# Six tile pairs of the feed-forward's shift segment: fetched in the output projection, multiplied at its norm

## The chip, the cores and the metric

The kernel runs on one core of one Trainium2 chip. A core has TensorE (PE), VectorE (DVE), ScalarE (ACT), GpSimd (POOL) and SyncE (SP), each with its own instruction stream, 16 DMA engines shared by all queues, a working memory (SBUF) and accumulation banks (PSUM, 8 banks of 512 fp32 for each partition). Engines wait for each other only through semaphores. The metric is device time in microseconds (us).

## The reference

Two transformer blocks over 256 tokens of width 2048, one after the other. In the first one, a vector c sets six rows of 2048 numbers (`mod`), of which the fourth is the shift of the feed-forward's norm:

```python
silu_c = jax.nn.silu(c)
mod = silu_c @ w_ada[l] + b_ada[l]
shift_m, scale_m, gate_m, shift_f, scale_f, gate_f = jnp.split(mod, N_MOD, axis=-1)
h = modulate(rmsnorm(x, g_norm_mix[l]), shift_m, scale_m)
proj = h @ w_in[l]
...
mix = jnp.concatenate([o_diff, o_mla], axis=-1) @ w_out[l]
x = x + gate_m[:, None, :] * mix
h = modulate(rmsnorm(x, g_norm_ffn[l]), shift_f, scale_f)
f = jnp.square(jax.nn.relu(h @ w_ff1[l])) @ w_ff2[l]
x = x + gate_f[:, None, :] * f
```

`modulate(h, shift, scale)` is `h * (1 + scale) + shift`. `w_ada` is 2048 x 12288 fp32, 16 tiles of 128 rows; one segment (one of the six rows) is 16.8 MB. The second block has the same form with two other attentions, and its own `w_ada`.

## The kernel before

**Weights in chunks.** Every projection's weights come in chunks of 128 x 1024 fp32 (0.52 MB, two row tiles by 512 columns), numbered through the whole kernel. SP loads chunk n into `raw` (4 buffers) once VectorE has taken chunk n-4 apart; ScalarE rounds it to `hi` (L724), VectorE makes `lo` = raw - hi (L1178), each 4 buffers deep; TensorE multiplies hi and lo with the activations in three products (L2116 to L2118, 24 matmuls for a chunk of four column tiles). ScalarE takes chunk n apart when TensorE has used chunk n-4.

**Stages around the change.** Chunks 32 to 47 give the differential attention's values, 48 to 55 the query latent, 56 to 63 the key latent (narrower: 18 matmuls a chunk), 64 to 71 the query projection, 72 to 75 keys and values, 76 to 107 the output projection (`out1`, 32 chunks p = 0 to 31, in two halves of four column groups), and from 108 the first feed-forward. Between the chunks stand the steps of the attention, as `hooks` of a chunk: scores, exponentials, probabilities, transposes, products with the values. `turn` and `diff_turn` (L2427) are transposes on TensorE.

**The modulation rows.** A segment is silu(c) times 16 row tiles. It is computed in one of two ways. As a *pair* (`ada_pair` on SP, `pair` on TensorE, L2360): the tile's two halves of 128x1024 are loaded and TensorE multiplies them by silu(c), widened to 32 equal columns (`silu_wide`), in four matmuls side by side on the array, each with 32 output rows and 512 columns; in fp32 each becomes two records, so that a pair is 8 records. Or in *halves* on VectorE (`ada_half`, `scale_ada`, L1526 and L1675: multiply by a column and add), whose 128 partial sums TensorE adds up at the end (`sum_halves` L2368, `sum_rows` L2261). Segment 2 (the gate) is 16 pairs, beside chunks 24 to 45. Segment 3 (the shift of the feed-forward) is 20 halves of its first 10 tiles on VectorE (chunks 37 to 55), and six pairs for its last 6 tiles, behind chunks 47, 50, 53, 56, 59 and 62; all of it gathers in PSUM bank 6, from where ScalarE copies the row, four transposes turn it into columns (`turn_rows`), and VectorE adds the bias (`finish_row`). Segment 4 (the scale) is 32 halves on VectorE, `scale_ada(p + 6)` at chunk p of `out1`; SP loads them one behind each chunk (`scale_half`). The order is written out by hand, in tables keyed by chunk number (`pair_after`, `halves_after`, `hooks`).

**The norm before the feed-forward.** Behind the last chunk of `out1`, VectorE adds the last four tiles to x, ScalarE squares them (L782), TensorE sums them over the columns (`piece_stats`, L2554), ScalarE copies (L787), TensorE gathers two columns (`gather_stats`, L2562), VectorE and ScalarE take the inverse root, VectorE spreads it on a diagonal (L1365), TensorE turns it into rows (`spread_root`, L2697), and VectorE and ScalarE make the normed and shifted activations in six pieces (`norm_split`: L1394, L823, L1388). While TensorE waits, it is given idle products (`idle_products`, L2101, 128x512 of constants, two records each) and runs of waits that are already fulfilled (`line_pad`, L2106).

GpSimd clears three accumulators in `work` (L693) and `y` (L695), and then loads the tiles of segment 5 onward (L621), which VectorE multiplies beside the feed-forward (L1203).

## Time and profile before

| | us |
|---|---|
| median of 3 runs (lowest, highest) | 2586.71 (2582.69, 2593.8) |
| the profiled execution | 2587.24 |
| its span, first to last instruction | 2585.6 |
| TensorE busy (matmul) | 2512.2 (97%) |
| VectorE busy | 1957.8 (76%) |
| ScalarE busy | 1141.6 (44%) |
| GpSimd busy | 182.5 (7%) |

The span was run at a mean granted clock of TensorE of 0.994 of full speed. The profile shows each matmul with its start and a modelled end; matmuls overlap, so the time of a matmul on the path is the distance of two starts (0.11 us for 128x256 at full clock), not its duration. A busy engine is not always the one that sets the end: for that the chain of waits is read, which goes back from the last instruction through what released each step.

### The profile page before, as it was taken

Reading aid. Unit: us, or ns where it says so; the run is one execution under the profiler, and the core shown is the slowest. Engines: PE = TensorE matmul, PEld = TensorE weight load, DVE = VectorE, ACT = ScalarE, POOL = GpSimd, SP = SyncE. Lnnn points to the kernel's source line nnn. Section 1 sums busy time; section 2 is a strip of 40 time slices with the busy share of each in tenths; the row PEclk is TensorE's granted clock in tenths of the full one; section 3 lists DMA queues with packets and bytes.
Section 4 is the critical chain, followed back from the end, with each engine's and each line's share of the span. In section 5 each row is a group of like instructions: output and inputs, shape, how many; then the busy total and the mean of one; then the engine's idle time right before and its main releaser. Section 6 shows DMA issues by size and latency. Waiting matters only on the chain.

```text
span 2585.6 us, 45165 instructions
## 1 busy us (share of the span) xinstructions
PE 2512.2 (97%) x17142; PEld 2266.0 (88%) x17142; DVE 1957.8 (76%) x2056; ACT 1141.6 (44%) x1335; POOL 182.5 (7%) x288
## 2 busy tenths in 40 slices
PE   6999999999999999999999999999989999999997
PEld 4777889789989988998999999999969898898986
DVE  4567799788887887889868979888777566575665
ACT  3334544444444444444434444544454444444443
POOL 5200000200100010100000000001010000000000
PEclk8999999999999999999999999999999999999999
DMA  9999868689889887885867765578847676676764
GB/s 369 386 321 347 298 227 270 211 284 313 300 301 302 292 304 238 294 305 189 262 210 237 237 213 170 172 257 286 273 154 244 205 240 226 211 243 217 225 216 139
DMA packets 312769, 658.64 MB, mean 255 GB/s; under 512 B 31367, under 2 KB 37790, under 8 KB 312382
## 3 DMA queue, kind: packets, MB, share of 16 engines
q1 hardware_dynamic: 279712, 539.04, 61.7%
q0 software_dynamic: 32480, 117.56, 13.8%
q8 instruction: 93, 1.52, 0.2%
q10 hardware_dynamic: 446, 0.21, 0.0%
q14 instruction: 38, 0.31, 0.0%
HBM read 654.62 MB, written 2.10 MB: 254 GB/s over the span
## 4 chain that ended last, share of the span: by engine, by line
PE 79%; DVE 9%; DMA 6%; ACT 3%; issue 2%; SPq 1%; DVEq 0%; ACTq 0%
PE ps L2145 18%; PE ps L2116 9%; PE ps L2117 9%; PE ps L2146 9%; PE ps L2118 9%; PE ps L2193 6%; PE ps L2195 6%; PE ps L2194 6%; DMA raw<-in_w_ff 3%; DVE lo L1178 3%; DMA raw<-in_w_in 2%; DVE work L1203 1%; ACT hi L724 1%; PE ps L2360 1%; DVE proj L1394 1%
## 5 line engine op out<-in xcount | busy, mean ns | idle before, releaser
L1178 DVE TENSOR_TENSOR lo<-raw,hi 128x1024 fp32r<-128x1024 f32 (+2 forms) x868 | 1038.8, 1212 | 512.4 <-ACT hi L724 509.6
L724 ACT ACTIVATE hi<-raw 128x1024 fp32r<-128x1024 f32 (+2 forms) x868 | 901.6, 1049 | 1156.0 <-PE ps L2118 401.8
L2145 PE MATMUL ps<-acts,hi 128*128 128x512 f32 x2048 | 673.4, 383 | 7.9 <-DVE lo L1178 5.5
L2116 PE MATMUL ps<-acts,hi 128*128 128x256 f32 x2384 | 669.5, 281 | 10.7 <-DVE acts L1513 4.7
L2117 PE MATMUL ps<-acts,hi 128*128 128x256 f32 x2384 | 658.0, 276 | 0.0
L2118 PE MATMUL ps<-acts,lo 128*128 128x256 f32 x2384 | 657.7, 276 | 0.0
L2146 PE MATMUL ps<-acts,lo 128*128 128x256 f32 x2048 | 558.2, 273 | 0.0
L2116 PEld LDWEIGHTS ps<-acts,hi 128*128 128x128 f32 x2384 | 458.1, 192 | 43.1 <-issue 35.0
L2117 PEld LDWEIGHTS ps<-acts,hi 128*128 128x128 f32 x2384 | 458.3, 192 | 1.5 <-issue 1.0
L2118 PEld LDWEIGHTS ps<-acts,lo 128*128 128x128 f32 x2384 | 458.5, 192 | 0.2
L2145 PEld LDWEIGHTS ps<-acts,hi 128*128 128x128 f32 x2048 | 387.0, 189 | 65.6 <-DVE lo L1178 7.5
L2146 PEld LDWEIGHTS ps<-acts,lo 128*128 128x128 f32 x2048 | 393.2, 192 | 0.3 <-issue 0.2
L2145 PE MATMUL ps<-f_acts,hi 128*128 128x512 f32 x768 | 252.2, 382 | 4.1 <-DVE lo L1178 4.1
L2146 PE MATMUL ps<-f_acts,lo 128*128 128x256 f32 x768 | 209.3, 273 | 0.0
L2193 PE MATMUL ps<-hi,f_acts 128*128 128x512 f32 x512 | 195.1, 381 | 0.0
L2194 PE MATMUL ps<-lo,f_acts 128*128 128x512 f32 x512 | 194.0, 379 | 0.0
L2195 PE MATMUL ps<-hi,f_acts 128*128 128x512 f32 x512 | 194.0, 379 | 0.0
L1203 DVE SCALAR_TENSOR_TENSOR work<-ada_ring,silu,work 128x1024 f32<-128x1024 f32 (+1 forms) x150 | 191.8, 1279 | 0.0
L2145 PEld LDWEIGHTS ps<-f_acts,hi 128*128 128x128 f32 x768 | 145.1, 189 | 25.2 <-DVE lo L1178 5.0
L621 POOL DMA_DIRECT2D ada_ring<-in_w_ada x128 | 68.0, 531 | 1208.1 <-DVE work L1203 1196.4
L2146 PEld LDWEIGHTS ps<-f_acts,lo 128*128 128x128 f32 x768 | 147.4, 192 | 0.0
L2193 PEld LDWEIGHTS ps<-hi,f_acts 128*128 128x128 f32 x512 | 96.8, 189 | 14.9 <-DVE lo L1178 0.8
(311 smaller groups left out, 2445.6 us busy)
## 6 DMA issues: line engine op xcount, KB each, us to landing
raw<-in_w_ff SPq DMA_DIRECT2D x512, 512.0 KB, 4.7
raw<-in_w_in SPq DMA_DIRECT2D x232, 512.0 KB, 4.7
ada_ring<-in_w_ada POOLq DMA_DIRECT2D x150, 512.0 KB, 5.5
proj<-in_w_ada SPq DMA_DIRECT2D x98, 512.0 KB, 8.9
proj<-in_w_ada POOLq DMA_DIRECT2D x64, 512.0 KB, 5.4
ada_ring<-in_w_ada SPq DMA_DIRECT2D x38, 512.0 KB, 6.5
raw<-in_w_out SPq DMA_DIRECT2D x32, 512.0 KB, 5.8
raw<-in_w_o SPq DMA_DIRECT2D x32, 512.0 KB, 5.6
```

The costliest lines, as they stand in the source:

```text
L621: pool.dma_start(ring[u][:, :], w[row, seg * D + u * half:seg * D + (u + 1) * half]).then_inc(landed[u], 16)
L724: nc.scalar.activation(hi[n % SPLIT][:, 0:k], raw[n % RAW][:, 0:k], ACT.Copy).then_inc(hi_ready, 1)
L1178: V.tensor_tensor(lo[n % SPLIT][:, 0:k], raw[n % RAW][:, 0:k], hi[n % SPLIT][:, 0:k].bitcast(F32), ALU.subtract)\
L1203: V.scalar_tensor_tensor(part, tile[:, :].unsqueeze(1), col, part, ALU.mult, ALU.add).then_inc(ada_used, 1)
L2116: M(out, h, right_hi, start=start, stop=False)
L2117: M(out, h, right_lo, start=False, stop=False)
L2118: return M(out, l, right_hi, start=False, stop=stop)
L2145: M(out[:, j, :], h[:, t, js], both, start=k == 0, stop=False)
L2146: last = M(out[:, j, 0:S], l[:, t, js], moved(src[:, k, 0:S]), start=False, stop=k == KT - 1)
L2193: M(out(t), xh, moved(hw), start=start, stop=False)
L2194: M(out(t), xh, moved(lw), start=False, stop=False)
L2195: last = M(out(t), xl, moved(hw), start=False, stop=stop)
```

## The change

The six pairs of segment 3 leave the latent projections. Their tiles are now loaded whole (128x2048, 1.05 MB, one transfer each) on SP's queue into parts of `proj` that are free by then: tile 0 behind chunk p = 4 of `out1`, tiles 1, 2 and 3 behind p = 18, 20 and 22, and tiles 4 and 5 behind p = 31, once the last half of the scale segment is used (`ada_used`). TensorE multiplies them at the norm before the feed-forward: two pairs where two idle products stood ahead of the last column sums, one before the gather, three before the spread, then four transposes of the summed row and one idle product where three stood. Their sum goes to PSUM bank 0 (`LATE_BANK`); ScalarE copies it to `mod_rows`, the transposes go to bank 1, and VectorE adds the 16 columns to `mods`, where the first ten tiles' share and the bias already are. VectorE's first norm piece and ScalarE's wait for that sum (`late_ready`). VectorE writes `silu_wide` a second time at p = 17, since its place in `work` has been used in between. The row of segment 4 is copied to `work` rather than to `proj[8:10]`. GpSimd clears the accumulators in the order 0, 2, 1, the last one when the transposes are done. `sum_halves` starts its bank instead of adding to it.

```diff
-        SUM_ROWS = {4: proj[:, 8:10, :], 8: proj[:, 48:50, :], 9: work[:, 0, 0:NC], 10: work[:, 0, 0:NC], 11: work[:, 0, 0:NC]}
+        SUM_ROWS = {4: work[:, 3, 0:2 * S].rearrange("p (a n) -> p a n", a=2), 8: proj[:, 48:50, :], 9: work[:, 0, 0:NC], 10: work[:, 0, 0:NC], 11: work[:, 0, 0:NC]}
...
-        pair_after = {(24 + 21 * p // 15 if p < KT else 47 + 15 * (p - KT) // (KT - MOVED - 1)): p for p in range(2 * KT - MOVED)}
+        pair_after = {24 + 21 * p // 15: p for p in range(KT)}
+        LATE = KT - MOVED
+        late_tiles = [proj[:, a:a + 8, :].rearrange("p t n -> p (t n)") for a in (0, 32, 40, 24, 16, 8)]
+        late_issued = {4: (0,), 18: (1,), 20: (2,), 22: (3,), 31: (4, 5)}
...
+            def late_pair(p):
+
+                if p == 0:
+                    sp.wait_ge(dn_normed, 2)
+                elif p < 3:
+                    sp.wait_ge(scored, 12)
+                elif p == 3:
+                    sp.wait_ge(pv_done, 6)
+                else:
+                    sp.wait_ge(ada_used, ADA * 5 * KT)
+                k = MOVED + p
+                sp.dma_start(late_tiles[p], w_ada[0][k * P:(k + 1) * P, 3 * D:4 * D]).then_inc(late_pair_landed[p], 16)
...
                 if 2 <= p < 2 * KT - 4:
                     scale_half(p + 4)
+                for q in late_issued.get(p, ()):
+                    late_pair(q)
...
-                    for a in range(3):
+                    for a in (0, 2, 1):
+                        if a == 1:
+                            pool.wait_ge(late_turned, 1)
                         nc.gpsimd.memset(ada_acc(a), 0.0).then_inc(acc_cleared, 1)
...
             root(tok(0), tok(1))
+            act.wait_ge(late_used, LATE)
+            nc.scalar.activation(mod_rows, ps[:, LATE_BANK, :], ACT.Copy).then_inc(late_copied, 1)
             act.wait_ge(mod_ready, 3)
+            act.wait_ge(late_ready, 1)
             norm_split("ffn", shift=3)
...
+            def silu_columns():
+                V.tensor_copy(silu_wide[:, :, :], silu[:, 0:KT].unsqueeze(2).to_broadcast([P, KT, 32])).then_inc(wide_ready, 1)
...
             dve.wait_ge(mod_ready, 3)
+            dve.wait_ge(late_turned, 1)
+            shifts_3 = mods[:, 3 * KT:4 * KT].rearrange("p (j c) -> p j c", c=4)
+            V.tensor_tensor(shifts_3, shifts_3, ps[:, LATE_BANK + 1, :].rearrange("p (c j n) -> p n j c", c=4, j=4)[:, 0], ALU.add).then_inc(late_ready, 1)
+            dve.wait_ge(late_ready, 1)
             dve.wait_ge(rs_spread, 1)
             norm_split("ffn", xT, ffn_scale[0], lambda t: mod(3, t), ps[:, 5, 0:S])
...
                 pe.wait_ge(half_used, HALVES)
+                pe.wait_ge(rows_copied, 1)
                 for j in range(4):
-                    last = M(ps[32 * j:32 * j + 32, 6, :], ones[:, 0:32], half_sum[j // 2][:, (j % 2) * NC:(j % 2 + 1) * NC], start=False, stop=False)
-                last.then_inc(ada_used, HALVES)
+                    last = M(ps[32 * j:32 * j + 32, 6, :], ones[:, 0:32], half_sum[j // 2][:, (j % 2) * NC:(j % 2 + 1) * NC], start=True, stop=True)
+                last.then_inc(ada_used, HALVES + ADA * LATE)
...
-            idle_products(2)
+            def late_pair(p):
+
+                pe.wait_ge(late_pair_landed[p], 16)
+                if p == 0:
+                    pe.wait_ge(wide_ready, 2)
+                    pe.wait_ge(group_out, first["out1"][1] + OUT1[-1][0])
+                for j in range(4):
+                    last = M(ps[32 * j:32 * j + 32, LATE_BANK, :], silu_wide[:, MOVED + p, :], late_tiles[p][:, j * NC:(j + 1) * NC],
+                             start=p == 0, stop=p == LATE - 1)
+                last.then_inc(late_used, 1)
+
+            late_pair(0)
+            late_pair(1)
             line_pad(80)
             piece_stats("ffn", 3)
+            late_pair(2)
             gather_stats("ffn")
-            idle_products(2)
+            for p in range(3, LATE):
+                late_pair(p)
             line_pad(32)
             spread_root(ps[:, 5, 0:S])
-            idle_products(3)
+            pe.wait_ge(late_copied, 1)
+            for c in range(4):
+                last = nc.tensor.transpose(ps[:, LATE_BANK + 1, c * P:(c + 1) * P], mod_rows[:, c * P:(c + 1) * P], ident)
+            last.then_inc(late_turned, 1)
+            idle_products(1, LATE_BANK)
             line_pad(32)
```

How instructions stand in a row, on three engines. TensorE in the key latent, at the transposes behind which the sixth pair stood; first the kernel before (L2427 the transposes, L2360 the pair, L2116 the next chunk's first product):

```order
L2118 MATMUL ps<-acts,lo 128x256
L2427 MATMUL ps<-consts_sb,work 128x128 [waits probs_ready]
L2427 MATMUL ps<-consts_sb,work 128x128 x3
L2360 MATMUL ps<-ada_ring,work 32x512 [waits pair_landed0]
L2360 MATMUL ps<-ada_ring,work 32x512 x3
L2116 MATMUL ps<-acts,hi 128x256 [waits lo_ready]
```

In the changed kernel, where these lines are numbered 31 or 32 higher (L2458 the transposes, L2148 to L2150 the products), the chunk follows the transposes:

```order
L2150 MATMUL ps<-acts,lo 128x256
L2458 MATMUL ps<-consts_sb,work 128x128 [waits probs_ready]
L2458 MATMUL ps<-consts_sb,work 128x128 x3
L2148 MATMUL ps<-acts,hi 128x256 [waits lo_ready]
L2149 MATMUL ps<-acts,hi 128x256
L2150 MATMUL ps<-acts,lo 128x256
```

The pair's four matmuls are gone, and nothing else moved there. TensorE at the norm, from the last product of the output projection to the feed-forward's first, before (L2101 idle products, L2554 column sums, L2562 gather, L2697 spread, L2145 the first product):

```order
L2118 MATMUL ps<-acts,lo 128x256
L2101 MATMUL ps<-consts_sb 128x512 x2
L2554 MATMUL ps<-proj,consts_sb 32x256 [waits consts_landed,tile_squared]
L2554 MATMUL ps<-proj,consts_sb 32x256 [waits tile_squared] x3
L2562 MATMUL ps<-consts_sb,work 128x1 [waits stat_copied]
L2562 MATMUL ps<-consts_sb,work 128x1
L2101 MATMUL ps<-consts_sb 128x512 x2
L2697 MATMUL ps<-work,consts_sb 128x256 [waits consts_landed,rs_diagonal]
L2101 MATMUL ps<-consts_sb 128x512 x3
```

And in the changed kernel (L2737 the late pairs, L2585 column sums, L2593 gather, L2728 spread, L2753 transposes of the row, L2133 the idle product):

```order
L2737 MATMUL ps<-proj,work 32x512 [waits late_pair_landed1]
L2737 MATMUL ps<-proj,work 32x512 x3
L2585 MATMUL ps<-proj,consts_sb 32x256 [waits consts_landed,tile_squared]
L2585 MATMUL ps<-proj,consts_sb 32x256 [waits tile_squared] x3
L2737 MATMUL ps<-proj,work 32x512 [waits late_pair_landed2]
L2737 MATMUL ps<-proj,work 32x512 x3
L2593 MATMUL ps<-consts_sb,work 128x1 [waits stat_copied]
L2593 MATMUL ps<-consts_sb,work 128x1
L2737 MATMUL ps<-proj,work 32x512 [waits late_pair_landed3]
L2737 MATMUL ps<-proj,work 32x512 x3
```

Ahead of these rows stands the first pair, behind them the fifth and sixth; then:

```order
L2728 MATMUL ps<-work,consts_sb 128x256 [waits consts_landed,rs_diagonal]
L2753 MATMUL ps<-consts_sb,work 128x128 [waits late_copied]
L2753 MATMUL ps<-consts_sb,work 128x128 x3
L2133 MATMUL ps<-consts_sb 128x512
L2779 UNCONDITIONAL_BRANCH [waits consts_landed]
```

Seven idle products have become six pairs, four transposes and one idle product. SP at the end of the output projection, in the changed kernel (L516 halves of the scale segment, L475 weight chunks, L468 late pairs, L581 the start of the feed-forward's loops):

```order
L516 DMA ada_ring<-in_w_ada 128x1024 [waits ada_used]
L475 DMA raw<-in_w_out 128x2x512 [waits lo_ready] x4
L468 DMA proj<-in_w_ada 128x2048 [waits ada_used] x2
L580 UNCONDITIONAL_BRANCH
L581 UNCONDITIONAL_BRANCH
L581 ISA
L475 ISA [waits lo_ready]
L475 DMA raw<-in_w_ff 128x2x512
```

Two loads with a wait of their own now stand between the last chunk of the output projection and the first of the feed-forward; before, the four chunks were followed by the branch.

## Rows read from the trace of the kernel before

**Rows 1.** The page's part 4: shares of the chain that ended last, by engine

```profile
PE 79%; DVE 9%; DMA 6%; ACT 3%; issue 2%; SPq 1%; DVEq 0%; ACTq 0%
```

**Rows 2.** Windows: length, busy us of PE, PEld, DVE, ACT, POOL; clock, DMA share, GB/s

```profile
246.00:292.00 46.00, 46.00 (x368) 38.93 (x364) 38.97 (x52) 20.41 (x43) 0.00 (x0) 1.00 1.00 352
...
303.00:307.00 4.00, 4.00 (x23) 3.39 (x20) 3.15 (x4) 1.79 (x2) 0.00 (x0) 0.60 0.35 91
...
412.00:464.00 52.00, 52.00 (x468) 49.45 (x467) 45.71 (x54) 23.89 (x24) 6.05 (x4) 1.00 0.82 279
```

**Rows 3.** Chain of waits, 236 to 480 us: start us, us on the chain, what

```profile
269.18 0.99 PE ps L2360 x8
...
292.17 0.99 PE ps L2360 x8
...
295.47 0.85 ACT hi L724
...
302.32 1.36 PE ps L2360 x8
```

**Rows 4.** Timeline of VectorE: start us, us, line, operation, [idle before <- releaser]

```profile
268.68 0.18 DVE L1586 RECIPROCAL small<-small 128x4 f32<-128x4 f32 x1 [0.84 <-ACT work L894]
...
288.35 0.96 DVE L1178 TENSOR_TENSOR lo<-raw,hi 128x768 fp32r<-128x768 f32 x1 [2.01 <-ACT hi L724]
...
292.08 0.96 DVE L1178 TENSOR_TENSOR lo<-raw,hi 128x768 fp32r<-128x768 f32 x1 [0.86 <-ACT hi L724]
```

**Rows 5.** Timeline of TensorE at the transposes ahead of the sixth pair

```profile
301.66 0.66 PE L2427 MATMUL ps<-consts_sb,work 128*128 128x128 f32 x4 [1.83 <-DVE work L1595]
```

**Rows 6.** Timeline of TensorE at the norm before the feed-forward

```profile
463.85 1.88 PE L2101 MATMUL ps<-consts_sb 128*128 128x512 f32 x4
...
466.60 0.64 PE L2554 MATMUL ps<-proj,consts_sb 128*32 128x256 f32 x8 [0.88 <-ACT proj L782]
...
467.74 0.61 PE L2562 MATMUL ps<-consts_sb,work 128*128 128x1 f32 x4 [0.49 <-ACT work L787]
...
468.20 1.96 PE L2101 MATMUL ps<-consts_sb 128*128 128x512 f32 x4
...
470.17 0.67 PE L2697 MATMUL ps<-work,consts_sb 128*128 128x256 f32 x2
```

**Rows 7.** Timeline of ScalarE and VectorE at the same norm

```profile
465.07 1.32 ACT L782 ACTIVATE proj<-xT 128x256 f32<-128x256 f32 x4
...
470.96 0.87 DVE L1394 SCALAR_TENSOR_TENSOR proj<-xT,cols,ps 128x256 f32<-128x256 f32 x2 [0.93 <-PE ps L2697]
```

**Rows 8.** Instructions of L2106, 460 to 467.5 us; ns min/median/max, first and last start

```profile
L2106 PEldq EVENT_SEMAPHORE  x39: 51/51/51, 462.3 to 466.4; - x39
```

**Rows 9.** Instructions of L925 and L2270, the same columns

```profile
L925 ACT ACTIVATE proj<-ps x5: 572/597/598, 452.0 to 1191.5; 128x512 f32<-128x512 f32 x5
...
L2270 PE MATMUL ps<-consts_sb,proj x20: 272/273/273, 457.3 to 1195.9; 128*128 128x128 f32 x20
```

**Rows 10.** Timelines and landing times of L498, end of the output projection

```profile
446.33 52.26 SPq L457 DMA_DIRECT2D raw<-in_w_ff  x15
...
448.35 1.28 DVE L1675 SCALAR_TENSOR_TENSOR work<-ada_ring,silu,work 128x1024 f32<-128x1024 f32 x1
...
454.87 1.07 ACT L724 ACTIVATE hi<-raw 128x1024 fp32r<-128x1024 f32 x1 [2.31 <-PE ps L2118]
...
460.50 0.64 PE L2554 MATMUL ps<-proj,consts_sb 128*32 128x256 f32 x8
...
464.11 1.06 ACT L724 ACTIVATE hi<-raw 128x1024 fp32r<-128x1024 f32 x1 [2.39 <-PE ps L2118]
...
DMA to landing us min/median/max: 3.3/6.2/8.2
```

**Rows 11.** Timelines of GpSimd at the norm and of VectorE behind it

```profile
457.95 5.32 POOL L693 MEMSET work<- 128x2048 f32 x3 [376.21 <-PE ps L2270]
...
487.02 1.28 DVE L1203 SCALAR_TENSOR_TENSOR work<-ada_ring,silu,work 128x1024 f32 x1
```

More of the change, by code:

```diff
@@ L51 @@
 RING = 4
-SUM_AT = 57
 N_MOD = 6
@@ L315, in build @@
             tiles_issued[n] = tiles_issued.get(n, ()) + (u,)
-        pair_after = {(24 + 21 * p // 15 if p < KT else 47 + 15 * (p - KT) // (KT - MOVED - 1)): p for p in range(2 * KT - MOVED)}
-        PAIRS_AHEAD = sum(n < SUM_AT for n in pair_after)
+        pair_after = {24 + 21 * p // 15: p for p in range(KT)}
+        LATE = KT - MOVED
+        late_tiles = [proj[:, a:a + 8, :].rearrange("p t n -> p (t n)") for a in (0, 32, 40, 24, 16, 8)]
+        late_issued = {4: (0,), 18: (1,), 20: (2,), 22: (3,), 31: (4, 5)}
+        late_pair_landed = [sem(f"late_pair_landed{i}") for i in range(LATE)]
+        late_used, late_copied, late_turned, late_ready = (sem(n) for n in ("late_used", "late_copied", "late_turned", "late_ready"))
         halves_after = {37: (0,), 38: (1,), 39: (2,), 41: (3, 4), 45: (5, 6), 46: (7, 8), 47: (9, 10), 49: (11, 12), 51: (13,),
@@ L390, in build @@
         out1_done = [max(p for p, (h, r, c) in enumerate(OUT1) if r == q) for q in range(4)]
+        LATE_BANK = 2 * ((first["out1"][1] + OUT1[-1][0] + 1) % 2)
         X2_BANKS = ((0, 1), (2, 3), (0, 1), (6, 7))
@@ L480, in ada_pair @@
                     last = p - PAIRS + 1
-                    sp.wait_ge(ada_used, ADA * (2 * KT + last) + (HALVES if last > PAIRS_AHEAD else 0))
-                seg, k, half = 2 + p // KT, p if p < KT else p - KT + MOVED, D // ADA
+                    sp.wait_ge(ada_used, ADA * (2 * KT + last))
+                seg, k, half = 2, p, D // ADA
                 for u in range(2):
@@ L1797, in _ @@
             ffn_scale = []
-            hooks.update({29: lambda: finish_row(4), 30: third_sum})
+            def silu_columns():
+                V.tensor_copy(silu_wide[:, :, :], silu[:, 0:KT].unsqueeze(2).to_broadcast([P, KT, 32])).then_inc(wide_ready, 1)
+            hooks.update({17: silu_columns, 29: lambda: finish_row(4), 30: third_sum})
             for p, (g, q, c) in enumerate(OUT1):
@@ L2351, in pair @@
             def pair(p):
-                seg, k = 2 + p // KT, p if p < KT else p - KT + MOVED
+                k = p
                 pe.wait_ge(pair_landed[p % PAIRS], 32 * (p // PAIRS + 1))
@@ L2356, in pair @@
                     pe.wait_ge(mods_block, BLOCKS)
-                if p == KT:
-                    pe.wait_ge(rows_copied, 1)
                 for j in range(4):
                     last = M(ps[32 * j:32 * j + 32, 6, :], silu_wide[:, k, :],
-                             pair_tiles[p % PAIRS][j // 2][:, (j % 2) * NC:(j % 2 + 1) * NC], start=p in (0, KT), stop=k == KT - 1)
+                             pair_tiles[p % PAIRS][j // 2][:, (j % 2) * NC:(j % 2 + 1) * NC], start=k == 0, stop=k == KT - 1)
                 last.then_inc(ada_used, ADA)
```

## The prediction

> **What bounds the kernel now.** The page first: the chain that ended last runs on TensorE for 79% and on VectorE for 9% [rows 1], so an edit pays where it takes work off TensorE and nothing else is late in its place. All times below are on the clock of the kernel before.
>
> Next the windows [rows 2]. From 246 to 292 us TensorE has no free time (46.00 of 46.00) and the 16 DMA engines none either (share 1.00 at 352 GB/s). From 412 to 464, the second half of the output projection, TensorE is again full and DMA is at 0.82.
>
> Then the chain of waits from 236 to 480. Four of the six pairs that the change moves lie on it at 0.99 or 1.00 us as in the first row of [rows 3] (they start at 245.41, 258.07, 269.18 and 280.97), the fifth at 292.17 too, the sixth at 302.32 with 1.36 us at a lower clock: 6.35 us together. Between the fifth and the sixth the chain leaves TensorE: ScalarE's split of chunk 60 at 295.47, the exponentials, VectorE's probabilities, and TensorE's transposes at 301.66 after a wait of 1.83 [rows 3, 5]. At the norm (464 to 471) it goes ScalarE's squares, column sums, gather, idle products, spread, and from 470.96 VectorE's norm pieces [rows 6, 7].
>
> **Six pairs out of the latent projections.** If TensorE alone were late, 6.35 us would go. But the transposes at 301.66 wait for VectorE, and VectorE gets earlier only where it stands waiting for something that gets earlier. [rows 4] shows where. At 268.68 it waits for exponentials queued on ScalarE behind the split of chunk 56, which TensorE's chunk 52 releases; two removed pairs precede that, so this point moves by 2.0. From there to 288.35 VectorE is busy with its shares of the segment, whose loads follow its own progress; at 288.35 it waits for a split that stands behind exponentials that VectorE itself released. So 2.0 is kept, no more. At 292.08 the wait of 0.86 was for TensorE's chunk 59, which is now earlier by more than that: it goes. ScalarE's split at 295.47 stood about 0.2 behind the root before it, and that goes. Sum: 2.0 + 0.86 + 0.2 = 3.0 us at 301.66, not 5.0; TensorE's wait there grows from 1.83 to about 3.8.
>
> The sixth pair stood behind these transposes. Taking it away gives at most its 1.36. After it comes chunk 63 (18 matmuls, 2.0 us at full clock), which ran in the stretch with a mean granted clock of 0.60 [rows 2]: full speed is 1.00, the half level 0.50. It comes 4.36 earlier and after a longer pause, so more of it may run at the half level. I take 0.95 of the 1.36, which leaves **3.95 us** gained when the query projection begins; the ends are 3.0 (the clock takes it all) and 6.35 (VectorE follows TensorE after all). TensorE's four column sums of the halves keep their place and get one wait more, long satisfied.
>
> **The way to the norm.** Up to the end of the output projection every engine's work follows TensorE's, and the shift is kept. Added on the way: the silu columns on VectorE, 128x512, about half of the 1.28 of a 128x1024 row [rows 10], under TensorE's full stretch: VectorE is busy for 45.7 of 52 there [rows 2]. Six loads of 1 MB each move to SP's queue. The first four are issued between chunks; 1.05 MB at 352 GB/s is 3.0 us each in a stretch with 0.18 to spare, and the rings in front of ScalarE and VectorE are several chunks deep, so I cost them at nothing.
>
> The last two are different. They stand behind chunk 31's load and wait for the last use of the scale segment, which ends at 448.35 + 1.28 = 449.63 [rows 10]. Queued behind them on SP is the first weight chunk of the feed-forward, which was issued at 446.33. It now goes out at about 450.5 behind 2.1 MB: 2.62 MB at 352 GB/s is 7.4 us, and 1.8 for the start (a 0.52 MB load lands in 3.3 at best, 1.5 of it transfer): landed at about 458.9. ScalarE took it at 454.87, so it stops for some 4 us, with the squares of the third piece behind it. TensorE wants their column sums at 460.50 [rows 10]; they are ready at 458.9 + 1.06 + 1.06 = 461.0. That costs TensorE 0.4. ScalarE and VectorE catch up by 464.11, where ScalarE's last split waits for TensorE anyway. Ends: 0 and 4. I take **0.4 us lost**.
>
> **The norm.** Two idle products (1.88) before the last column sums become two pairs (2.0): equal. But the 80 padding waits follow them. They take 51 ns each, 4.1 us, and ran from 462.3 to 466.4 [rows 8], beside matmuls issued earlier: when they began, the four idle matmuls of 463.85 [rows 6] and 14 before them (1.55 us at 0.11) were still to start, 18 in all. Two pairs are 16 matmul records against the products' 4, so the padding begins about when the first pair does, at 463.7, and ends at 467.8. ScalarE's squares end at 466.4 [rows 7]; the column sums come at 467.95 instead of 466.60: 1.35 late. The third pair then holds the gather: sums from 467.95 to 468.45, pair to 469.45, gather to 470.05 (before: 468.35). Three more pairs: 473.05 (before, two idle products filled the wait for VectorE until 470.17). Behind the last pair a new chain replaces the spread as what VectorE waits for: ScalarE's copy, 0.60 [rows 9]; four transposes, 0.60 (0.273 each, overlapped) [rows 9]; VectorE's add, 0.17; four hand-overs of about 0.07. 473.05 + 1.65 = 474.7 for the first norm piece against 470.96 [rows 7]: **3.75 us lost**. Bounds: 2.4 if the padding stays hidden, 4.3 if each hand-over takes 0.2.
>
> Queued behind the new waits: on ScalarE the first norm pieces; on GpSimd the third clearing, the clearing of y and the loads of the next segment. One clearing is 5.32 / 3 = 1.8, that of y 3.5, so these loads go at about 480 and land by 487; VectorE's first use was at 487.02 [rows 11] and is now at 490.8. Covered, by some 3 us. The rest of the feed-forward starts from VectorE's last norm piece and follows it.
>
> **Sum.** -3.95 + 0.4 + 3.75 = +0.2 us on the profiled execution's 2587.24 (span 2585.6); against the median of 2586.71 it is 2586.9. I say 2587.0.
>
> **Rivals.** (a) The padding stays hidden behind the pairs, because many more matmuls can be queued than I read: then the column sums stay at 466.60 and the loss at the norm is 2.4; total -1.15, 2585.6. For it: the waits have no dependence on the pairs. Against: when the padding began 18 matmuls stood ahead of it, and it began no earlier. The Trainium skill, "TensorE: Matmul & The Clock Gate", section "Architectural detail: the array is 16× 32×32, not 1× 128×128", gives TensorE a queue of 64; by that rule both pairs would fit and this rival would hold; the trace speaks for some 36 entries, weight loads and matmuls counted.
>
> (b) VectorE follows TensorE fully, because DMA (share 1.00 from 246 to 292) is relieved of 6 MB and its shares of the segment land earlier: the gain is 5 to 6.35 and the total -1 to -2.2, 2585; with (a) 2583.5. Against: only one wait of about 1.2 us of VectorE there was for a load.
>
> (c) Slower: the loads in the output projection. 4.2 MB more fall into 412 to 464, 11.9 us of transfer where 9.4 are free. If the last two land so late that the chunk behind them comes after 461 instead of 458.9, each further us goes straight into ScalarE, the piece's squares and TensorE; a span of 3 to 5 us gives 2590 to 2592. It decides from about 2 us of extra landing time. For it: SP's queue is blocked from 443 to 449.6 and then three loads start at once. Against: nothing else is in flight at that moment but the tail of chunk 31.
>
> (d) The moved work doesn't lie in the pause but makes it long: the start of the feed-forward meets its transfers differently, or the lower clock spreads over the query projection (another stretch like that of 303 to 307, 0.60 instead of 1.00 over 4 us, costs 1.6 [rows 2]); 5 to 15 us, 2592 to 2602.
>
> **How the numbers follow.** Forecast 0.50 with its own range 2584.5 to 2589.5; (a) 0.15; (b) 0.13; (c) 0.15; (d) 0.07. Gain and loss nearly cancel, and every case but the far end of (d) is small against 0.5% (12.9 us), about what a measurement of this kernel can tell from no change: faster 0.02, same 0.94, slower 0.04. The range, 2582 to 2592, takes in (a), (b) and most of (c).
>
> **What would show it.** The six pairs as about 1.0 us each between the last output matmuls and the spread; the wait before the transposes near 298 grown to 3 to 4 us, and a half clock behind it; VectorE's first norm piece 3.5 to 4 us further from the last output matmul than the 7.1 of before; ScalarE waiting some 4 us for the first feed-forward chunk. Wrong if the padding ends before the squares (a), if the transposes come 5 us earlier (b), or if TensorE waits over 1 us for the third piece's squares (c).

## The result and the profile after

| | before | changed |
|---|---|---|
| median (lowest, highest), us | 2585.68 (2580.12, 2593.8) | 2592.07 (2587.0, 2600.93) |
| profiled execution, us | 2587.24 | 2593.8 |
| its span, us | 2585.6 | 2592.1 |

The ratio is 1.0022 with the interval 1.0014 to 1.0031: 6.4 us slower by the medians, 3.6 to 8.0 by the interval. The forecast was 0.3 us slower than the median of before. 0.22% is inside the 0.5% that was forecast as most likely, but 2592.07 lies at the very edge of the stated range (2582 to 2592) and outside the forecast's own (2584.5 to 2589.5): the sum is off by 6 us by the profiled executions, and the rest looks for them.

A shift of this size is read by place. I took the start of VectorE's subtraction for the same chunk (L1178 before, L1203 after) in both traces. The two executions already differ by 1.33 us at chunk 48, ahead of the first moved pair, so this is taken off everywhere:

| after minus before, less 1.33, us | measured | forecast |
|---|---|---|
| chunk 64, behind the transposes near 300 | -3.57 | -3.0 |
| chunk 68, query projection | -5.12 | -3.95 |
| chunks 76 to 96, up to the middle of the output projection | -4.45 | -3.95 |
| chunk 107, its last chunks | +0.22 | -3.95 |
| chunk 112, feed-forward | +5.98 | +0.2 |
| last instruction | +5.24 | +0.2 |

Single traces of one kernel scatter here: a second trace of the kernel before (c1_before, below) stands at +0.58 at chunk 64, -0.61 at chunk 68 and +0.3 from chunk 76 to 112, so the second row says little by itself. The gain was larger than forecast, and two losses follow: 4.7 us between chunks 96 and 107, where the forecast has none, and the norm.

**The gain.** TensorE's transposes behind the key latent, the line that answers to [rows 5], in the timeline of TensorE of the changed kernel (start us, us, engine, line, operation, tiles, idle before and its releaser):

```profile
299.06 0.66 PE L2458 MATMUL ps<-consts_sb,work 128*128 128x128 f32 x4 [1.84 <-DVE work L1620]
```

They come 2.60 earlier, 3.93 with the offset. The wait is still 1.8 and did not grow to 3.8. VectorE's timeline shows its waits on the way, beside [rows 4]:

```profile
279.08 1.29 DVE L1551 SCALAR_TENSOR_TENSOR proj<-proj,silu 128x1024 f32<-128x1024 f32 x1 [0.29 <-DMA proj<-in_w_ada]
...
286.44 0.96 DVE L1203 TENSOR_TENSOR lo<-raw,hi 128x768 fp32r<-128x768 f32 x1 [1.88 <-ACT hi L746]
...
289.85 0.96 DVE L1203 TENSOR_TENSOR lo<-raw,hi 128x768 fp32r<-128x768 f32 x1 [0.52 <-ACT hi L746]
```

The first of them, a share of the segment, waited 1.24 us for its load in the trace of before and now waits 0.29. It looks like rival (b), but the other traces don't bear that out. The second trace of the kernel before has only 0.24 there, and its transposes come 0.6 later, not earlier:

```profile
280.25 2.59 DVE L1526 SCALAR_TENSOR_TENSOR proj<-proj,silu 128x1024 f32<-128x1024 f32 x2 [0.24 <-DMA proj<-in_w_ada]
```

e10_before_no_pad, which is the kernel before up to the norm, has no such wait at all and its transposes where the first trace has them; e6_norm_only, without the pairs, waits 1.26 for a load and still has them 3.84 earlier. What the traces agree on is the sum of VectorE's waits between its subtraction for chunk 56 and the transposes: 5.7, 5.6 and 5.6 us in the three with the six pairs, 3.6 in both traces of the changed kernel and 3.4 to 3.9 in e4_none and e6_norm_only. Two waits for exponentials (0.84 and 0.28 in the trace of before) are gone in all of the latter; most of the rest is waits for ScalarE's splits. So VectorE gained some 2 us of waiting, mostly for ScalarE, beyond what it had gained by chunk 56 (1.4 in the changed kernel, 1.6 in e4_none).

The windows (columns as in [rows 2]) show DMA in that stretch, and what became of the half clock of [rows 2]:

```profile
246.00:292.00 46.00, 45.01 (x362) 40.84 (x360) 42.05 (x56) 22.04 (x44) 0.00 (x0) 1.00 0.80 263
303.00:307.00 4.00, 3.91 (x27) 3.74 (x28) 3.30 (x5) 1.99 (x4) 0.00 (x0) 1.00 0.86 249
```

DMA fell from a share of 1.00 to 0.80, and the stretch behind the transposes ran at full clock instead of 0.60. In c1_before it ran at full clock too; there a half clock fell at 322.6. Behind chunk 63 TensorE has a new wait, for VectorE's activations of the query projection:

```profile
303.09 0.35 PE L2148 MATMUL ps<-acts,hi 128*128 128x256 f32 x1 [1.37 <-DVE acts L1402]
```

From the transposes to the first product behind chunk 64 it is 6.11 us in the changed kernel, and 6.11 in c1_before with the sixth pair (1.06) at full clock, where that wait is 0.17; in the first trace of before, at half clock, it is 7.30. So at full clock taking the sixth pair away gives nothing: TensorE waits for VectorE instead.

**The output projection.** The chain of waits there is no longer TensorE's own work (start us, us on the chain, what):

```profile
417.31 12.52 DMA raw<-in_w_out
...
429.86 1.07 ACT hi L746
...
432.10 1.28 DVE work L1700
...
434.98 1.06 ACT proj L797
```

A chunk of `w_out` issued at 417.31, directly behind the third late load (416.55), lands after 12.52 us. The issues of this line from 412 to 422 (duration ns, first and last start; then the landing times), first in the changed kernel, then in the kernel before:

```profile
L475 SPq DMA_DIRECT2D raw<-in_w_out x3: 378/379/1051, 413.9 to 421.2; - x3
...
DMA to landing us min/median/max: 10.9/11.2/12.5
```

```profile
L457 SPq DMA_DIRECT2D raw<-in_w_out x4: 367/368/368, 411.6 to 420.4; - x4
...
DMA to landing us min/median/max: 5.7/6.0/6.5
```

The same landing has doubled. The 16 engines are full: 0.97 from 403 to 417, then as in these windows of the changed kernel, where the kernel before had 0.95 from 416 to 436; in the second, TensorE's clock has fallen to half:

```profile
416.00:436.00 20.00, 16.84 (x151) 16.65 (x150) 16.51 (x22) 7.82 (x9) 0.00 (x0) 0.99 1.03 401
436.00:439.00 3.00, 2.91 (x17) 2.10 (x18) 3.00 (x4) 1.74 (x3) 0.00 (x0) 0.50 1.04 400
```

ScalarE waits for these loads four times, and TensorE in the end 3.24 us for the column sums of the second piece, which then take 1.08 instead of 0.64:

```profile
429.86 1.06 ACT L746 ACTIVATE hi<-raw 128x1024 fp32r<-128x1024 f32 x1 [2.54 <-DMA raw<-in_w_out]
...
459.51 1.07 ACT L746 ACTIVATE hi<-raw 128x1024 fp32r<-128x1024 f32 x1 [5.40 <-DMA raw<-in_w_ff]
```

```profile
436.09 1.08 PE L2585 MATMUL ps<-proj,consts_sb 128*32 128x256 f32 x8 [3.24 <-ACT proj L797]
```

The 5.40 at 459.51 is the wait that I had forecast at about 4, for the first feed-forward chunk behind the last two loads.

**The norm.** TensorE, the lines that answer to [rows 6]:

```profile
465.48 1.92 PE L2737 MATMUL ps<-proj,work 128*32 128x512 f32 x16
469.92 1.08 PE L2585 MATMUL ps<-proj,consts_sb 128*32 128x256 f32 x8 [2.51 <-issue]
470.75 1.96 PE L2737 MATMUL ps<-proj,work 128*32 128x512 f32 x8
472.64 0.85 PE L2593 MATMUL ps<-consts_sb,work 128*128 128x1 f32 x4
473.41 2.78 PE L2737 MATMUL ps<-proj,work 128*32 128x512 f32 x24
476.13 0.70 PE L2728 MATMUL ps<-work,consts_sb 128*128 128x256 f32 x2
476.91 0.66 PE L2753 MATMUL ps<-consts_sb,work 128*128 128x128 f32 x4
```

A pair takes 1.0 us (1.92 for two, 2.78 for three). Between the second pair and the column sums TensorE has nothing to do for 2.51 us, "issue" being the padding, whose waits take 51 ns each, as in [rows 8]. The first column sums come 4.44 behind the first pair. The sums and the third pair run at half clock: 1.08 for 0.64, 1.96 for 1.07 in a kernel below. ScalarE's copy and VectorE's addition and first norm piece:

```profile
476.26 0.60 ACT L1078 ACTIVATE work<-ps 128x512 f32<-128x512 f32 x1 [2.35 <-PE ps L2737]
```

```profile
477.68 0.17 DVE L1846 TENSOR_TENSOR mods<-mods,ps 128x16 f32<-128x16 f32 x1 [2.51 <-PE ps L2753]
477.89 0.87 DVE L1419 SCALAR_TENSOR_TENSOR proj<-xT,cols,ps 128x256 f32<-128x256 f32 x2
```

From the last product of the output projection to that piece it was 7.22 us (463.74 to 470.96), and is 12.61 (465.28 to 477.89): 5.39 lost, where 3.75 was forecast.

### The profile page after: what moved, and what is told of

It reads as the page before. It is cut to its first block, busy times and chain, and to the rows that moved or that the text cites. A ratio compares the mean times of both kernels' runs of the same rounds, so it can differ in the third digit from the quotient of the medians.

```text
span 2592.1 us, 45148 instructions
## 1 busy us (share of the span) xinstructions
PE 2509.4 (97%) x17134; PEld 2264.8 (87%) x17134; DVE 1957.3 (76%) x2058; ACT 1141.3 (44%) x1336; POOL 179.8 (7%) x288
## 4 chain that ended last, share of the span: by engine, by line
PE 82%; DVE 9%; DMA 4%; issue 2%; ACT 2%; SPq 0%; DVEq 0%; ACTq 0%
PE ps L2177 19%; PE ps L2148 10%; PE ps L2150 10%; PE ps L2149 10%; PE ps L2178 9%; PE ps L2225 6%; PE ps L2227 6%; PE ps L2226 6%; DVE lo L1203 2%; DMA raw<-in_w_ff 2%; ACT hi L746 1%; DVE work L1228 1%; DMA raw<-in_w_in 1%; PE ps L2344 1%; DVE proj L1419 1%
## 5 line engine op out<-in xcount | busy, mean ns | idle before, releaser
L1203 DVE TENSOR_TENSOR lo<-raw,hi 128x1024 fp32r<-128x1024 f32 (+2 forms) x868 | 1037.8, 1212 | 515.7 <-ACT hi L746 513.3
L2148 PE MATMUL ps<-acts,hi 128*128 128x256 f32 x2384 | 669.4, 281 | 14.2 <-DVE acts L1538 6.0
L2150 PE MATMUL ps<-acts,lo 128*128 128x256 f32 x2384 | 657.6, 276 | 0.0
L2148 PEld LDWEIGHTS ps<-acts,hi 128*128 128x128 f32 x2384 | 458.1, 192 | 43.2 <-issue 35.3
L2150 PEld LDWEIGHTS ps<-acts,lo 128*128 128x128 f32 x2384 | 458.4, 192 | 0.2
```

The costliest lines, as they stand in the source:

```text
L1203: V.tensor_tensor(lo[n % SPLIT][:, 0:k], raw[n % RAW][:, 0:k], hi[n % SPLIT][:, 0:k].bitcast(F32), ALU.subtract)\
L2148: M(out, h, right_hi, start=start, stop=False)
L2150: return M(out, l, right_hi, start=False, stop=stop)
```

## Experiments

Every kernel is read in two ways: by its times against the kernel before (ratio of the runs, with interval), and by its trace up to the norm. Shifts are against the first trace of before, each less its own offset at chunk 48.

| kernel | chunk 76 | chunk 96 | chunk 107 | last product to first norm piece | median us | ratio to before |
|---|---|---|---|---|---|---|
| before | 0 | 0 | 0 | 7.22 | 2585.7 | |
| c1_before | +0.32 | +0.30 | +0.30 | 7.22 | (one) 2584.4 | |
| changed | -4.44 | -4.46 | +0.22 | 12.61 | 2592.07 | 1.0022 [1.0014, 1.0031] |
| c2_after | -5.12 | -5.14 | -0.35 | 12.61 | (one) 2589.4 | |
| e4_none | -5.36 | -5.40 | -5.40 | 7.30 | 2584.3 | 0.9995 [0.9985, 1.0005] |
| e5_loads_only | -5.26 | -5.27 | -0.65 | 8.75 | 2587.52 | 1.0004 [0.9995, 1.0013] |
| e6_norm_only | -4.47 | -4.49 | -4.49 | 12.44 | 2588.3 | 1.0003 [0.9992, 1.0014] |
| e1_no_pad | -5.07 | -5.10 | -0.42 | 9.12 | 2585.48 | 1.0001 [0.9992, 1.0010] |
| e2_loads_moved | -5.29 | -5.30 | -5.30 | 11.03 | 2586.39 | 1.0004 [0.9993, 1.0015] |
| e3_both | -5.36 | -5.39 | -5.39 | 9.12 | 2581.24 | 0.9978 [0.9969, 0.9987] |
| e9_add_behind | -4.78 | -4.80 | -4.51 | 8.18 | 2580.56 | 0.9979 [0.9970, 0.9989] |
| e10_before_no_pad | -0.02 | -0.04 | -0.04 | 7.02 | 2583.59 | 0.9990 [0.9980, 0.9999] |
| e11_pads_spread | -4.78 | -4.80 | -4.80 | 9.12 | 2581.78 | 0.9980 [0.9967, 0.9992] |
| e12_none_no_pad | -5.29 | -5.31 | -5.31 | 7.02 | 2580.02 | 0.9976 [0.9967, 0.9986] |

### The gain alone

```diff
-                for q in late_issued.get(p, ()):
-                    late_pair(q)
```

and the norm (TensorE, ScalarE, VectorE, GpSimd) as before.

> The changed kernel with the six pairs in neither place: their loads and their multiplications are left out (so six tenths of the shift's sum over 16 tiles is incomplete: tiles 10 to 15 are missing), and the norm is as in the kernel before. This is the gain alone. The forecast's step says 3.95 us below the kernel before (2581.7 against 2585.7). The trace of the changed kernel, read by chunks, says 4.45 (2581.2), with the wait before the transposes near 298 grown. The rival that VectorE follows TensorE in full says 5 to 6.35 (2579.3 to 2580.7).

The trace shows 5.40 us of gain, kept without loss from chunk 76 to 107. The rival's size (5 to 6.35) was nearer than my step's. The transposes near 298 come at 297.50 against 301.66, with the same wait:

```profile
297.50 0.66 PE L2447 MATMUL ps<-consts_sb,work 128*128 128x128 f32 x4 [1.83 <-DVE work L1613]
```

4.16 is VectorE's gain. The rest, 1.2, is the half clock that is missing behind it: from the transposes to the first product behind chunk 64 it is 7.30 in the first trace of before, 6.11 here and 6.11 in c1_before. Against c1_before the gain at the transposes is 4.75 and at chunk 76 5.7, of which 0.9 is that trace's own half clock at 322.6. The times however show only 1.3 us (interval 3.9 faster to 1.3 slower), less than every expectation. I come back to that under the padding.

### The loads alone

The six loads stay where the change has them; nothing uses them. GpSimd waits for them before it clears `y`, which lies in the same memory.

> As e4_none, but with the six 1.05 MB loads where the change has them; nothing multiplies them (tiles 10 to 15 are still missing from the shift). Theory of the loads: the three issued at p = 18, 20 and 22 delay the output projection's own chunks, 4.5 to 5 us above e4_none (2586), with ScalarE waiting for DMA at 425 to 438 and TensorE's column sums idle for about 3 us near 433. The forecast's step says that the loads cost 0 to 0.4 in all (2581.7): then the delay in the changed kernel's trace was a chance of that one execution.

Theory of the loads: from chunk 96 to 107 this kernel loses 4.62 us, the changed kernel 4.68. Its chain shows the same chunk, issued behind the third load:

```profile
415.29 12.34 DMA raw<-in_w_out
...
427.66 1.07 ACT hi L746
```

The forecast's "at nothing" falls. At the norm of before, the last two loads cost too, 8.75 against 7.30: ScalarE's squares are late there, the sums wait 0.95, and half clock stretches the idle products behind the gather (3.66 for four instead of 1.96):

```profile
466.16 0.64 PE L2578 MATMUL ps<-proj,consts_sb 128*32 128x256 f32 x8 [0.95 <-ACT proj L804]
467.29 0.61 PE L2586 MATMUL ps<-consts_sb,work 128*128 128x1 f32 x4 [0.49 <-ACT work L809]
467.76 3.66 PE L2126 MATMUL ps<-consts_sb 128*128 128x512 f32 x4
```

So by the trace the loads cost 6.2 us up to chunk 112 here (4.6 and 1.45), by the times only 3.2 against e4_none. It may lie in e4_none, whose times are some 4 us slower than its trace says; that stays open.

### The norm alone

```diff
-                pe.wait_ge(late_pair_landed[p], 16)
```

and no loads.

> As e4_none, but with the multiplications, copy, transposes and addition at the norm as in the change, on whatever stands in those parts of memory, since the loads are left out (the shift is wrong in its part from tiles 10 to 15). The norm alone. The forecast's step says 3.75 above e4_none (2585.4); read from the changed kernel's trace it is 5.3 (2586.5), of which about 1.5 by the half clock behind the padding's pause. If most of the loss is the loads' and not the norm's, it is under 2.5 above e4_none.

12.44 against 7.30: 5.1 us, as the changed kernel's trace had it; by the times 4.0. The half clock fell at 463.5 here, again at the padding's pause. Loads (3.2) and norm (4.0) together are 7.2 above e4_none by the times; the changed kernel is 7.8 above it. That closes, but weakly: each of these differences of medians is uncertain by some 3 us, and all three lean on e4_none. By the traces at chunk 112 it is 6.2 and 6.1 against 10.9: 1.45 of the loads' cost vanishes behind the pairs.

### The norm without the padding

```diff
             late_pair(1)
-            line_pad(80)
             piece_stats("ffn", 3)
```

> The changed kernel without the 80 padding waits between the second pair and the last column sums. Theory of the padding: these waits hold the column sums back by 1.7 us and let the clock fall, so without them it is 1.7 to 3 us faster than the change (2589 to 2590.4), the column sums following the second pair at once, at full clock. Rival: the column sums wait for ScalarE's squares or for the pairs anyway, and nothing moves (within 0.5).

More than expected: 6.6 us below the change by the medians, 3.49 at the norm (9.12 against 12.61), and no half clock there. The column sums follow the second pair. Here TensorE in e3_both, whose norm is the same:

```profile
458.55 1.92 PE L2737 MATMUL ps<-proj,work 128*32 128x512 f32 x16
460.29 1.17 PE L2585 MATMUL ps<-proj,consts_sb 128*32 128x256 f32 x7
...
462.46 0.61 PE L2593 MATMUL ps<-consts_sb,work 128*128 128x1 f32 x4
463.00 2.78 PE L2737 MATMUL ps<-proj,work 128*32 128x512 f32 x24
```

The sums start 1.74 behind the first pair, not 4.44, because nothing keeps TensorE from them: the first of ScalarE's four squares is ready (it ended at 460.08), and the sums follow the others one by one. The chain is now six pairs, the copy, the transposes and the addition.

### The loads behind other chunks

```diff
-        late_issued = {4: (0,), 18: (1,), 20: (2,), 22: (3,), 31: (4, 5)}
+        late_issued = {4: (0,), 15: (1,), 16: (2,), 28: (3,), 30: (5,), 31: (4,)}
...
                 else:
-                    sp.wait_ge(ada_used, ADA * 5 * KT)
+                    sp.wait_ge(ada_used, ADA * 4 * KT + (30 if p == 4 else 28))
```

> The changed kernel with the same six loads behind other chunks of the output projection: tiles 1 and 2 behind p = 15 and 16 (390 to 410 us, where the kernel before has a DMA share of 0.70 and 0.54), tile 3 behind p = 28, tile 5 behind p = 30 and tile 4 behind p = 31, the last two now waiting only for the halves of the scale segment that stood in their own place. The 80 padding waits stay. Theory of the loads: no chunk takes more than 9 us to land, TensorE's wait of 3 us before the column sums near 433 goes, and its last matmul of the output projection comes 4 to 4.7 us earlier; the time is 3 to 5 us below the change's 2592.07 (2587 to 2589). Rival: any six loads of 1 MB cost the same there, wherever they are issued, since DMA is full in the sum (2591 to 2592).

From chunk 96 to 107 nothing is lost any more (-5.30 to -5.30), and the chunks of 412 to 422 land as in the kernel before:

```profile
L475 SPq DMA_DIRECT2D raw<-in_w_out x3: 378/379/787, 415.1 to 421.3; - x3
...
DMA to landing us min/median/max: 5.7/6.4/6.6
```

It is the same 6.3 MB in the same projection, so the rival (any place costs the same) falls. The loads are issued at 387.7, 391.0, 430.6, 435.3 and 438.4 (tile 0 is earlier in both), and fill windows that had room. Windows of this kernel; before, the first had a share of 0.70 and the second 0.66:

```profile
390.00:400.00 10.00, 10.00 (x92) 10.00 (x92) 6.77 (x12) 6.26 (x13) 0.00 (x0) 1.00 0.93 347
...
440.00:450.00 10.00, 10.00 (x90) 8.51 (x89) 8.52 (x10) 5.14 (x6) 0.00 (x0) 1.00 1.03 401
```

The second window is as full as the changed kernel's was, 1.03 at 401 GB/s, and costs nothing. The weight chunks issued at 437.2 and 441.3 land in 8.2 and 8.0 us; in the changed kernel DMA was full from 403 to 436, and landings rose from 5.9 to 12.5 us. So a full share by itself is not what costs; it cost where it lasted until the chunks came too late.

The times: 5.7 us below the change, 0.6 more than expected at best. This kernel also gives my norm its test at full clock. The padding still leaves TensorE idle for 2.47 us, but the clock did not fall there:

```profile
462.96 0.64 PE L2585 MATMUL ps<-proj,consts_sb 128*32 128x256 f32 x8 [2.47 <-issue]
463.39 1.07 PE L2737 MATMUL ps<-proj,work 128*32 128x512 f32 x8
```

The windows behind that pause, in this kernel and in the changed one:

```profile
463.00:466.00 3.00, 3.00 (x32) 1.37 (x36) 0.63 (x4) 0.59 (x2) 0.00 (x0) 1.00 0.40 146
```

```profile
470.00:473.00 3.00, 3.00 (x18) 0.93 (x18) 0.00 (x0) 0.38 (x1) 0.00 (x0) 0.50 0.38 143
```

11.03 against 7.22 is 3.81 us lost, where 3.75 was forecast. By its parts: the column sums come 1.74 later behind the last product than in before (1.35 forecast), and from there to the norm piece it is 2.07 longer (2.40 forecast). The other 1.58 of the changed kernel is the half clock.

### Both

> The loads as in e2_loads_moved and no padding waits behind the second pair. If both causes are right and independent: 4.1 (padding, from the changed kernel without padding) and 3 to 4.7 (loads) below the change, 2583 to 2585, which is 1 to 3 us below the kernel before. If the two overlap (the squares of the last piece being late for either reason), only the larger goes: 2585 to 2587.

2581.24 us, lower than either theory had it: 10.8 below the change and 4.7 below the kernel before (ratio 0.9978, interval 0.9969 to 0.9987). The two single edits brought 5.7 and 6.6: nearly independent. It beats both kernels, but not all of it is the moved work's: the kernel before also gets faster without its padding (2583.59, e10_before_no_pad below), and against that it is 2.3 us.

### The addition behind the first norm piece

```diff
                     last.then_inc(normed, 1)
+                    if q == 0 and first:
+                        first()
```

where `first` is the wait for the transposes and the addition, no longer ahead of `norm_split`.

> e3_both, and VectorE adds the late columns behind its first norm piece instead of ahead of it (the first piece does not need the shift). VectorE's first piece then no longer waits for the copy and the transposes; ScalarE's first piece still waits for the sum. Expected: 0.3 to 0.5 us below e3_both at the norm, which the times cannot tell and the trace can. If VectorE's inverse root and not the chain of copy and transposes comes last, nothing moves.

```profile
467.10 0.48 DVE L1419 SCALAR_TENSOR_TENSOR proj<-xT,cols,ps 128x256 f32<-128x256 f32 x1 [1.78 <-PE ps L2731]
467.76 0.17 DVE L1850 TENSOR_TENSOR mods<-mods,ps 128x16 f32<-128x16 f32 x1 [0.18 <-PE ps L2755]
```

The first piece starts 8.18 behind the last product instead of 9.12, twice what was expected. From chunk 107 to 112 this kernel loses 1.37 us and e3_both 2.28. 2580.56 against 2581.24 can't be told apart by the times, as expected.

### The two kernels once more

> The kernel before once more, for a second trace: how much of a shift read by chunks between two executions is the execution's and not the edit's. Up to the first feed-forward (chunk 108) the two should agree within 1.5 us, all of it from the start of the kernel. In the feed-forward, where the traces so far part by up to 8 us between chunk 112 and 372 in both directions, either they agree (then these differences are made by the edits) or they part by 2 us or more (then they are chance, and the times' scatter of 2580 to 2594 comes from there).

Once its offset of 1.18 is off, it agrees with the first trace within 0.6 us at chunks 64, 68, 76, 96, 107 and 112. From chunk 112 to 372, in the feed-forward, it gains 4.89 on it. That is chance, not an edit: shifts at the end of single traces say nothing below some 5 us here, and everything above is therefore read up to chunk 112.

> The changed kernel once more, for a second trace. From the last product of the output projection to VectorE's first norm piece its first trace shows 12.61 us with the half clock behind the padding, and the kernel with the same norm but moved loads 11.03 at full clock. If the half clock there is chance, this one may show either: 11.0 with full clock, or 12.4 to 12.6 with half. The delay of about 4 us at chunks 97 to 99 of the output projection should be there again; if it is not, it was chance.

All of it is there again: 4.79 us lost from chunk 96 to 107 with a wait of 3.33 before the column sums, and 12.61 at the norm with the half clock:

```profile
435.12 1.08 PE L2585 MATMUL ps<-proj,consts_sb 128*32 128x256 f32 x8 [3.33 <-ACT proj L797]
```

```profile
468.95 1.08 PE L2585 MATMUL ps<-proj,consts_sb 128*32 128x256 f32 x8 [2.47 <-issue]
```

### The padding by itself

> The kernel before without its own 80 padding waits ahead of the last column sums. In its trace they end together with ScalarE's squares (466.4), so by the trace they cost nothing and it stays at 2585.6 (within 1). Rival: the times of the kernels without padding lie 1 to 3 us lower than their traces say up to the feed-forward, and those with it higher, so the padding costs something beyond the norm (the place of the code behind it, or a half clock in most executions): then this one is 2 to 4 us faster than the kernel before (2582 to 2583.6).

> e4_none (the six pairs in neither place, tiles 10 to 15 missing from the shift) without the 80 waits as well. By the traces alone it equals e4_none (2584.3 by its times, 2580.6 by its trace's shift of 5 us up to the feed-forward). If padding costs beyond the norm, 2 to 4 us below e4_none (2580 to 2582).

> e3_both with the 80 waits put back, but 16 each behind chunks p = 16, 19, 22, 25 and 28 of the output projection, where 18 queued products of 0.11 us (2 us) cover 16 waits of 51 ns (0.8 us). The code behind is again as long as in the change. If it matters where the waits stand: as e3_both (2581.2), the norm at 9.1 us. If it matters that they are there (the length of the code): as e2_loads_moved, 2585 to 2587.

| with the 80 waits | without | by the medians | at the norm in the traces |
|---|---|---|---|
| before 2586.37 | e10_before_no_pad 2583.59 | 2.8 | 0.20 |
| e4_none 2584.3 | e12_none_no_pad 2580.02 | 4.3 | 0.28 |
| changed 2592.07 | e1_no_pad 2585.48 | 6.6 | 3.49 |
| e2_loads_moved 2586.39 | e3_both 2581.24 | 5.2 | 1.91 |

The rival of e10 holds: the kernel before was faster without its own padding (ratio 0.9990, interval 0.9980 to 0.9999), although there its trace shows only 0.2 us in them. In all four pairs the times show some 3 us (2.6 to 4.0) more than the norm does, though each difference of medians is itself uncertain by some 3 us, and the kernels of the second and third pair were not timed together. e11_pads_spread has the same 80 waits at other places and is as fast as e3_both (2581.78), with 9.12 at the norm, so what matters is where they stand, not how long the code is. Where these 3 us lie was not shown. The traces' feed-forward scatters too much to tell: from chunk 112 to 372 they shift by -5.8 to 0 with padding at the norm and by -9.4 to -0.5 without. It may also be that the half clock falls at the pause in more executions than in the traced ones. The granted clocks of the single runs speak softly against it where there is no long pause: 2.6 and 4.0 us lost at half clock would lower the mean by 0.0010 and 0.0015, and it is 0.9924 and 0.9922 for the kernel before and e10_before_no_pad, 0.9922 and 0.9924 for e4_none and e12_none_no_pad. For e2_loads_moved and e3_both (0.9918 and 0.9929) they leave it room. Where the time goes stays open, and with it why e4_none is no faster than 2584.3 by its times.

## Why the prediction was right or wrong

**Pairs of about 1.0 us at the norm: right.** 1.92 for two, 2.78 for three.

**The gain: the mechanism was right, the size was not.** VectorE and not TensorE set the transposes near 300, but the step "2.0 is kept, no more" failed. It held up to 277 (1.98 by chunk 59). Then VectorE's waits, mostly for ScalarE, shrank further: from chunk 56 to the transposes by some 2 us in all. Rival (b) had the size, but its cause, a load of VectorE's own share, is not borne out: that wait is 1.24, 0.24 and none in three traces of kernels with the pairs, without moving their transposes earlier. Which wait for ScalarE brings how much was not tested. And the step from 4.36 to 3.95 failed in both its terms: the sixth pair's 1.36 is worth nothing at full clock, where TensorE waits 1.37 for VectorE's activations instead, and the stretch that I took to run more at half clock had none. What is gained there, 1.2, is the half clock of one trace; the other traces of kernels with the pairs have theirs at 322, and some without them at 316 to 319. -3.95 measured -4.45 and -5.12 in two traces of the changed kernel, -5.4 in e4_none.

**The first four loads "at nothing": wrong, and the largest error.** 4.7 us, shown by leaving the loads in alone (4.62) and by moving them (0.00). I compared what they need, 3.0 us each, with the share 0.82 of 412 to 464. That is a mean over a stretch of two kinds: from 416 to 436 the kernel before already had 0.95,

```profile
416.00:436.00 20.00, 20.00 (x183) 19.88 (x186) 20.00 (x23) 10.39 (x11) 0.00 (x0) 1.00 0.95 343
```

and the free time lay behind 440. The change issues three loads between 403 and 417, ahead of the full stretch. Rival (c) had late chunks as the mechanism and the price (2590 to 2592), but at the wrong two loads: that its price fits is luck.

**The last two loads, 0.4: right by their effect, for a partly wrong reason.** ScalarE waits 5.40 for the chunk behind them (about 4 forecast). The sum had 461.0 against 460.50, which is 0.5 and not 0.4. TensorE loses nothing by it in the changed kernel, since the squares are hidden behind the pairs: 9.12 in e1_no_pad with these loads and 9.12 in e3_both with others. Under the norm of before they would have cost 1.4 (e5_loads_only).

**The norm, 3.75: right at full clock, and then 1.6 of half clock.** 3.81 in e2_loads_moved (padding 0.4 dearer, the chain behind it 0.3 cheaper than forecast), 5.39 in the changed kernel. The 80 waits start at 465.5, with the first pair, and the column sums come 4.4 us later, as worked out from the queue. So rival (a), that they stay hidden, falls; about 16 matmul records and their weight loads stood ahead of them. The Trainium skill ("TensorE: Matmul & The Clock Gate", "Architectural detail: the array is 16× 32×32, not 1× 128×128") gives TensorE a queue of 64; the trace does not agree, counted in weight loads and matmul records. By a queue of 64 of them 16 more products would stand ahead, and the waits would have begun and ended some 1.8 us earlier (an estimate, 16 times 0.11 us). What I left out is that a pause of 2.5 us can bring an interval of some 3 us at half clock, although [rows 2] had shown me such an interval behind a shorter one. It came with seven of the eight pauses of over 2.4 us that stand in these traces between chunk 48 and the feed-forward (a ninth, 2.63 us at 1083.6 in e5_loads_only, had none), and no kernel without padding at the norm has one there.

**GpSimd's loads: right.** VectorE's first share of the next segment starts at 494.33 without a wait.

**The sum.** -3.95 + 0.4 + 3.75 was forecast; -4.45 + 4.68 + 5.39 and 0.4 behind the first norm piece is +6.0, of which the times show 6.4. The gain was taken 0.5 us too small, the loads 4.3 and the norm 1.6 to 2 too cheap: the sum near zero rested on two costs left out. That the time stayed within 0.25% of before is no merit of the working: each of these terms is small against the 0.5% that counted as no change.

## What to carry to other kernels

A moved load is costed in the window into which it falls, at the time at which it is issued, and not by the mean share of a stage: three loads of 1 MB cost 4.7 us when issued ahead of a stretch with a share of 0.95 (403.8, 410.1 and 416.6), and nothing when issued 14 to 19 us earlier or later (387.7, 391.0 and 430.6). Where work is put into a pause, look at what the pause is filled with already: padding waits that ended just in time behind short work become the longest thing on the path behind long work, and the idle time they make can bring the half clock with it. And a wait that differs between two kernels' traces is a cause only if a second trace of the same kernel doesn't differ as much: the load wait of 1.24 us was 0.24 in the next trace of the kernel before.

## What the runs showed of the hardware

- With DMA at a share of 1.03 (401 GB/s) from 416 to 436, and full before it, a 0.52 MB load took 10.9 to 12.5 us to land, against 5.7 to 6.5 for the loads issued at the same place (412 to 422) where the share was 0.95. Where it had been at 0.98 and then went to 1.03 (e2_loads_moved, 440 to 450), it took 8.0 to 8.2 and nothing was lost.
- The granted clock fell to 0.50 for some 3 us at TensorE's pauses of 3.0 to 3.3 us near 435 in every trace that has them (changed, c2_after, e5_loads_only, e1_no_pad), and at the padding's pause of 2.4 to 2.5 us in three of four (changed, c2_after, e6_norm_only, not e2_loads_moved). It began between 0.5 us before the pause's end and 0.4 us behind it. In such an interval a pair takes 1.96 us instead of 1.07.
- 80 fulfilled waits in TensorE's stream ahead of the norm cost about 3 us more in the times than the trace shows at their place, in four pairs of kernels, for a reason that stays open; the same waits among the products of the output projection cost nothing that can be measured.
